# Two attention phases of a hybrid layer: score units in another order, and inverse roots spread over partitions by transposes

## The chip, the cores and the metric

The kernel runs on one core of a Trainium2 chip. The metric is the device time of one execution in microseconds (us); the time of a kernel is the median of its runs. The engines are called as in the profile: PE (TensorE matmuls), PEld (its weight loads), DVE (VectorE), ACT (ScalarE), POOL (GpSimd) and SP (SyncE, which issues the DMAs).

## The reference

One decoder layer over 16 meta tokens and 1024 real tokens, float32: a half feed-forward network, a token mixer, a second half feed-forward network. The mixer has two causal attentions of 8 heads each, and the change is in these two alone:

```python
fq = rms_norm(split_heads(fq, FOX_HEADS), fox_q_norm)      # "fox": head dim 64
fk = rms_norm(split_heads(fk, FOX_HEADS), fox_k_norm)
o_fox = merge_heads(block_causal_attention(fq, fk, fv, log_f_cum)) @ w_branch_fox
...
q = rms_norm(q, mla_q_norm)                                # "mla": 64 + 32 rotary dims
k = rms_norm(k, mla_k_norm)
...
q = jnp.concatenate([q[..., :MLA_NOPE_DIM], rope(q[..., MLA_NOPE_DIM:], cos, sin)], axis=-1)
o_mla = merge_heads(block_causal_attention(q, k, v)) @ w_branch_mla
```

Softmax attention is `softmax(mask(q k^T * scale [+ forget terms])) v`; `rms_norm` multiplies by the inverse root of the mean square of a head's row.

## The kernel before

The layer is written as phases that follow one another: feed-forward network 1, a forget-gate phase, `fox_attention_phase`, `latent_attention_phase` (called MLA here), a gate phase and feed-forward network 2. Each engine has its own program of instructions in order, written out by hand, and engines wait for each other with semaphores (`wait`, `upto`). Float32 products are made of three matmuls on a high and a low part of each operand (`hi`, `lo`).

**Score units.** The scores of a head stand transposed, keys on partitions, queries along the free dimension. A unit is one tile of 128 keys (`kt`, 0 to 8) against one half of the queries (`c`, 0 or 1, 512 queries each), cut to the queries that may see these keys. So a head has `NW` = 14 units of unequal width `n`: for c = 0 widths 512, 400, 272, 144, 16 (kt 0 to 4), for c = 1 widths 512 five times (kt 0 to 4), then 400, 272, 144, 16 (kt 5 to 8). `ST_UNITS` is the list of them, and before it is in just this order. Both phases walk the list with index `w`.

For each unit: PE makes the scores (fox: `scores_open`, `scores_close`, L1921 to L1933; MLA: `scores`, L2435 to L2445; plus a mask matmul if the tile is on the diagonal), ACT takes the exponential (L1811, L2314), DVE rounds it to `p_hi` (L2091, L2601), POOL subtracts to get `p_lo` (L1733, L2250; in fox DVE does so itself for each fourth unit, `w % LO_DVE == 3`, L2094), and PE weighs the values with three matmuls (`weigh`, L1948 to L1950, L2459 to L2461) into the bank `OB[c]`, where a row of ones gives the denominator too. Fox has three score buffers and PE weighs unit w-3 at step w; MLA has two and weighs unit w-2 at step w. The first unit of a half (kt = 0) starts its bank, the last (`LAST_OF[c]`) closes it; some steps later ACT takes logarithm and exponential of the denominators (`rden`, L1817/L1819, L2320/L2322) and DVE multiplies (`o_fox` L2102, `o_mla` L2591).

**Fox** works on pairs of heads (4 pairs). A pair is first projected (6 units `u` of q and k, three groups of tokens, and 3 of v, L73 to L75), its maxima are found (`maxima`, L1905, DVE reduces them, L2048), then come its 2 x 14 score units.

**MLA** works on 8 heads, and preparation of head h+1 is woven into the 14 steps of head h: at steps 0 to 5 PE makes the projection `products(u)` (L2363 q, L2366 k), then the step's scores, then `weigh`, then `sums(u)` (L2376, sums of squares; waits for ACT's squares L2286/L2288) and, a step later, `broadcast(u)`. At steps 8 to 12 it makes the 14 maxima of the next head (L2418, reduced by DVE at L2554, two banks in turn), at step 13 it turns them and makes the values (L2398). The code of `prepare`:

```python
if w < NU:
    sums(p, h, w)
if 1 <= w <= NU:
    broadcast(p, h, w - 1)
maxima(p, h, w, 2)
```

**Inverse roots.** After `sums`, DVE scales (`ms`, L2514), ACT takes logarithm and exponential (L2295, L2297), POOL makes a Newton step of four small instructions (L2236 to L2242; fox L1714 to L1722). The root stands with tokens on partitions and is needed along the free dimension, the same on all partitions: `broadcast(u)` multiplies the column, repeated 128 times, by the identity `g.ident`, once for each of three tiles of 128 tokens (fox L1876, where POOL has written the repeated columns out in `r_wide`; MLA L2387, where the column is read with a stride of zero). ACT copies the result to `rs`, DVE scales q or k with it (L2027; L2525 to L2538) and they are split into hi and lo (L2545).

Of the kernel before, what the change touches and what calls it, by code (L numbers as in the profile page):

```python
# [23 lines left out]
P = 128  # L24
# [4 lines left out]
T = META + SEQ  # L29
# [35 lines left out]
REAL_TOKENS = [(META, 512), (META + 512, 512)]  # L65
# [1269 lines left out]

ST_UNITS = []
for _c, (_q0, _n) in enumerate(REAL_TOKENS):
    for _kt in range(9):  # L1340
        _a = max(_q0, P * _kt)
        if _a < _q0 + _n:
            ST_UNITS.append((_c, _kt, min(P * _kt, T - P), _a, _q0 + _n - _a))
NW = len(ST_UNITS)
LAST_OF = [max(w for w in range(NW) if ST_UNITS[w][0] == c) for c in range(2)]

# [240 lines left out]
def fox_attention_phase(nc, g):  # L1587
# [15 lines left out]
    with ExitStack() as s:  # L1603
# [12 lines left out]
        ms, r0, nt = sb("ms", [P, 2, 3 * NH]), sb("r0", [P, 2, 3 * NH]), sb("nt", [P, 2, 3 * NH])  # L1616
# [9 lines left out]
        PROJ, SUM, BC = (bank[0], bank[1], bank[4], bank[5]), bank[2], bank[6:8]  # L1626
# [201 lines left out]
        def _(pe):  # L1828
            def pair(p, last=False):
# [37 lines left out]
                def broadcast(u):  # L1867
                    c = units[u][1]
                    wait(pe, newton, p, 4 * NU, 4 * u + 4)
                    if u < 2:  # L1870
                        wait(pe, o_done, p, 4, 0)
                    else:
                        wait(pe, rs_done, p, NU, u - 1)
                    for i, off in enumerate(QK_TILES[c]):
                        r = r_wide[:, u % 2, NH * i:NH * i + NH, :].rearrange("p a b -> p (a b)")
                        last = nc.tensor.matmul(BC[u % 2][:, off:off + P], r, g.ident[:, :], start=True, stop=True)  # L1876
                    last.then_inc(bc_ready, 1)

                def values(b):
# [236 lines left out]
def latent_attention_phase(nc, g):  # L2116
# [14 lines left out]
    V_TILES = (range(0, 5), range(5, 9))  # L2131
    MAXIMA_FROM = NU + 2
    TURN_STEP, V_STEP = NW - 1, NW - 1
    FINISH_0, FINISH_1 = 7, 2

    ROPE_ROWS, SWAPPED = slice(NOPE, MLA_D), slice(MLA_D, P)
    with ExitStack() as s:
# [209 lines left out]
        def _(pe):  # L2347
# [32 lines left out]
            def broadcast(p, h, u):  # L2380
                upto(pe, newton, 4 * NU, p, h, 4 * u + 4)
                if u == 0:
                    upto(pe, v_done, 2, p, h, 0)
                else:
                    upto(pe, rs_done, NU, p, h, u)
                for i, off in enumerate(QK_TILES[units[u][1]]):
                    last = nc.tensor.matmul(BC[:, off:off + P], r0[:, u % 2, i:i + 1].broadcast_to([P, P]),  # L2387
                                            g.ident[:, :], start=True, stop=True)
                last.then_inc(bc_ready, 1)

            def values(p, h, b):
# [623 lines left out]
```

## Time and profile before

| | |
|---|---|
| median of 3 runs | 2602.05 us (2597.78 to 2606.18) |
| the profiled execution's own time | 2598.46 us |
| its span in the trace | 2596.3 us |
| mean granted clock of TensorE | 0.958 of full speed |
| PE / DVE / ACT / POOL busy | 94% / 55% / 37% / 21% of the span |

The own time is that of the execution that the profile shows; the span reaches from its first to its last instruction in the trace. The fox phase takes about the stretch from 780 to 1190 us, the MLA phase from 1190 to 1560 us. A head of MLA is one step list of 14; heads start at 1235.7, 1275.1, 1320.7, 1362.3, 1408.1, 1451.0, 1496.9 and 1539.1 us (the close of their first unit), and the last has no preparation beside it.

### The profile page before, as it was taken

Reading aid. Unit: us, or ns where it says so; the run is one execution under the profiler, and the core shown is the slowest. Engines: PE = TensorE matmul, PEld = TensorE weight load, DVE = VectorE, ACT = ScalarE, POOL = GpSimd, SP = SyncE. Lnnn points to the kernel's source line nnn. Section 1 sums busy time; section 2 is a strip of 40 time slices with the busy share of each in tenths; the row PEclk is TensorE's granted clock in tenths of the full one; section 3 lists DMA queues with packets and bytes.
Section 4 is the critical chain, followed back from the end, with each engine's and each line's share of the span. In section 5 each row is a group of like instructions: output and inputs, shape, how many; then the busy total and the mean of one; then the engine's idle time right before and its main releaser. Section 6 shows DMA issues by size and latency. Waiting matters only on the chain. (4 is left out here: it accounts for less than half of the span.)

```text
span 2596.3 us, 37171 instructions
## 1 busy us (share of the span) xinstructions
PE 2433.0 (94%) x14204; PEld 2152.8 (83%) x14204; DVE 1418.0 (55%) x2006; ACT 948.2 (37%) x1578; POOL 557.8 (21%) x655
## 2 busy tenths in 40 slices
PE   6999999999959999978999998999998999999999
PEld 6899999999958888976777777888876888887887
DVE  7665655565456567544666662111466666655553
ACT  5333333333344445432444443111334333334332
POOL 0023300000023344231444444222310333000000
PEclk8999999999979999987998998999999999999999
DMA  4365632565230000010000002111433566326653
GB/s 183 121 209 196 209 114 95 214 227 188 101 130 1 26 26 0 1 33 7 7 7 4 3 1 81 48 49 41 163 113 104 180 221 232 133 87 255 211 197 111
DMA packets 125908, 281.13 MB, mean 108 GB/s; under 512 B 9456, under 2 KB 56432, under 8 KB 122432
## 3 DMA queue, kind: packets, MB, share of 16 engines
q1 hardware_dynamic: 125760, 279.10, 31.0%
q8 instruction: 99, 1.62, 0.3%
q14 instruction: 49, 0.40, 0.0%
HBM read 198.60 MB, written 80.33 MB: 107 GB/s over the span
## 5 line engine op out<-in xcount | busy, mean ns | idle before, releaser
L1068 DVE TENSOR_TENSOR f_w_lo<-f_rw,f_w_hi 128x1024 fp32r<-128x1024 f32 x154 | 203.1, 1319 | 218.7 <-ACT f_w_hi L590 218.6
L833 PE MATMUL f_ps<-u_hi,f_w_hi 128*128 128x260 f32 (+1 forms) x1056 | 283.9, 323 | 26.5 <-DVE f_w_lo L1068 13.6
L833 PE MATMUL f_ps<-u_hi,f_w_lo 128*128 128x260 f32 (+1 forms) x1056 | 282.4, 322 | 0.0
L833 PE MATMUL f_ps<-u_lo,f_w_hi 128*128 128x260 f32 (+1 forms) x1056 | 282.4, 322 | 0.0
L590 ACT CAST f_w_hi<-f_rw 128x1024 fp32r<-128x1024 f32 x154 | 161.3, 1047 | 165.1 <-PE f_ps L833 148.7
L833 PE MATMUL f_ps<-f_far_hi,f_w_hi 128*128 128x260 f32 (+1 forms) x792 | 211.8, 322 | 8.7 <-DVE f_ev L1084 8.7
L833 PEld LDWEIGHTS f_ps<-u_hi,f_w_hi 128*128 128x128 f32 x1056 | 178.0, 192 | 43.1 <-DVE f_w_lo L1068 15.4
L833 PE MATMUL f_ps<-f_far_lo,f_w_hi 128*128 128x260 f32 (+1 forms) x792 | 210.9, 321 | 0.0
L833 PE MATMUL f_ps<-f_far_hi,f_w_lo 128*128 128x260 f32 (+1 forms) x792 | 210.8, 321 | 0.0
L833 PEld LDWEIGHTS f_ps<-u_lo,f_w_hi 128*128 128x128 f32 x1056 | 177.7, 191 | 14.2
L833 PEld LDWEIGHTS f_ps<-u_hi,f_w_lo 128*128 128x128 f32 x1056 | 177.6, 191 | 14.1
L73 PE MATMUL f_ps<-u_hi,f_w_hi 128*128 128x512 f32 x384 | 151.5, 394 | 9.4 <-POOL f_w_lo L2659 9.4
L75 PE MATMUL f_ps<-u_lo,f_w_hi 128*128 128x512 f32 x384 | 151.1, 393 | 0.0
L74 PE MATMUL f_ps<-u_hi,f_w_lo 128*128 128x512 f32 x384 | 151.1, 393 | 0.0
L833 PEld LDWEIGHTS f_ps<-f_far_hi,f_w_hi 128*128 128x128 f32 x792 | 132.8, 191 | 19.9 <-issue 9.6
L833 PEld LDWEIGHTS f_ps<-f_far_lo,f_w_hi 128*128 128x128 f32 x792 | 132.5, 190 | 10.6
L833 PEld LDWEIGHTS f_ps<-f_far_hi,f_w_lo 128*128 128x128 f32 x792 | 132.4, 190 | 10.4
L2761 DVE TENSOR_TENSOR f_sg<-f_ps,f_sg 128x512 f32<-128x512 f32 x32 | 22.1, 692 | 212.2 <-PE f_ps L75 203.4
L2250 POOL TENSOR_TENSOR mla_p_lo<-mla_p,mla_p_hi 128x512 fp32r<-128x512 f32 (+4 forms) x112 | 105.6, 943 | 69.5 <-DVE mla_p_hi L2601 69.5
L73 PE MATMUL fox_bank<-u_hi,fox_w_hi 128*128 128x384 f32 (+1 forms) x288 | 98.6, 342 | 16.1 <-DVE fox_w_lo L2007 15.9
L636 ACT CAST f_w_hi<-f_rw 128x1408 fp32r<-128x1408 f32 x36 | 49.5, 1376 | 171.6 <-PE f_ps L858 136.8
L2659 POOL TENSOR_TENSOR f_w_lo<-f_gt_raw,f_w_hi 128x1024 fp32r<-128x1024 f32 x27 | 66.5, 2467 | 198.0 <-ACT f_w_hi L2679 198.0
(385 smaller groups left out, 5987.1 us busy)
## 6 DMA issues: line engine op xcount, KB each, us to landing
f_rw<-in_gu SPq DMA_DIRECT2D x88, 512.0 KB, 4.4
f_rw<-kept_dsum SPq DMA_DIRECT2D x32, 704.0 KB, 4.9
f_rw<-kept_hid SPq DMA_DIRECT2D x33, 520.0 KB, 5.7
f_rw<-in_down SPq DMA_DIRECT2D x24, 704.0 KB, 4.1
f_rw<-kept_hid SPq DMA_DIRECT2D x33, 512.0 KB, 5.5
f_gt_raw<-in_gate SPq DMA_DIRECT2D x24, 512.0 KB, 3.5
h_in<-in_wd SPq DMA_DIRECT2D x11, 1024.0 KB, 7.2
kept_dsum<-h_in SPq DMA_DIRECT2D x44, 256.0 KB, 3.1
```

What stands on the lines that cost most here:

```text
L73: nc.tensor.matmul(out, w_hi, x_hi, start=first, stop=False)
L74: nc.tensor.matmul(out, w_lo, x_hi, start=False, stop=False)
L75: return nc.tensor.matmul(out, w_hi, x_lo, start=False, stop=last)
L590: nc.scalar.copy(slot(w_hi, st), src).then_inc(whi_done, 1)
L636: nc.scalar.copy(s_buf(near_hi, far_hi, w_hi, n), s_raw(n)).then_inc(shi_done, 1)
L833: last = nc.tensor.matmul(out[:, b, 0:N], w[:, c], u[:, b * N:(b + 1) * N], start=(j < 3 and k == 0 and i == 0), stop=(k == 3 and i == 2), ...
L1068: nc.vector.tensor_tensor(slot(w_lo, st), src, slot(w_hi, st).bitcast(F32), ALU.subtract).then_inc(wlo_done, 1)
L2250: nc.gpsimd.tensor_tensor(p_lo[:, w % 2, 0:n], p32[:, w % 2, 0:n], p_hi[:, w % 2, 0:n].bitcast(F32), ALU.subtract).then_inc(plo_done, 1)
L2659: nc.gpsimd.tensor_tensor(w_lo[:, j, :], raw[:, j, :], w_hi[:, j, :].bitcast(F32), ALU.subtract).then_inc(wlo_done, 1)
L2761: ins = nc.vector.tensor_tensor(sg[:, slot, :], bank[base + which][:, :], sg[:, slot, :], ALU.mult)
```

## The change

1. `ST_UNITS` gets a written-out order. Widths by step, before: 512, 400, 272, 144, 16, 512, 512, 512, 512, 512, 400, 272, 144, 16. After: 512, 400, 272, 512, 144, 512, 16, 512, 16, 512, 144, 512, 272, 400. `LAST_OF` goes from (4, 13) to (6, 13), and with it the finish of half 0: in MLA from step 7 to step 9 (`FINISH_0`), in fox from steps 8 and 22 of the 28 to steps 10 and 24.
2. Both `broadcast` functions issue `nc.tensor.transpose` of the repeated column in place of `nc.tensor.matmul` of it with the identity.

```diff
+ST_ORDER = [(0, 0), (0, 1), (0, 2), (1, 0), (0, 3), (1, 1), (0, 4), (1, 2), (1, 8), (1, 3), (1, 7), (1, 4), (1, 6), (1, 5)]
 ST_UNITS = []
-for _c, (_q0, _n) in enumerate(REAL_TOKENS):
-    for _kt in range(9):
-        _a = max(_q0, P * _kt)
-        if _a < _q0 + _n:
-            ST_UNITS.append((_c, _kt, min(P * _kt, T - P), _a, _q0 + _n - _a))
+for _c, _kt in ST_ORDER:
+    _q0, _n = REAL_TOKENS[_c]
+    _a = max(_q0, P * _kt)
+    ST_UNITS.append((_c, _kt, min(P * _kt, T - P), _a, _q0 + _n - _a))
...
-                        last = nc.tensor.matmul(BC[u % 2][:, off:off + P], r, g.ident[:, :], start=True, stop=True)
+                        last = nc.tensor.transpose(BC[u % 2][:, off:off + P], r, g.ident[:, :])
...
-    FINISH_0, FINISH_1 = 7, 2
+    FINISH_0, FINISH_1 = LAST_OF[0] + 3, 2
...
-                    last = nc.tensor.matmul(BC[:, off:off + P], r0[:, u % 2, i:i + 1].broadcast_to([P, P]),
-                                            g.ident[:, :], start=True, stop=True)
+                    last = nc.tensor.transpose(BC[:, off:off + P], r0[:, u % 2, i:i + 1].broadcast_to([P, P]),
+                                               g.ident[:, :])
```

## Rows read from the trace of the kernel before

**Rows 1.** The page's head and part 1: busy us of each engine.
```profile
span 2596.3 us, 37171 instructions
PE 2433.0 (94%) x14204; PEld 2152.8 (83%) x14204; DVE 1418.0 (55%) x2006; ACT 948.2 (37%) x1578; POOL 557.8 (21%) x655
```

**Rows 2.** Windows: length; PE, PEld, DVE, ACT, POOL busy; clock; DMA.
```profile
949.00:1004.50 55.50, 52.45 (x353) 50.42 (x352) 24.89 (x57) 23.50 (x60) 12.79 (x29) 1.00 0.09 29
915.20:949.00 33.80, 30.71 (x156) 25.04 (x154) 30.88 (x53) 18.94 (x39) 20.09 (x19) 0.95 0.01 1
1275.10:1320.70 45.60, 41.98 (x227) 34.59 (x226) 29.34 (x65) 19.23 (x51) 18.30 (x38) 0.89 0.02 4
1320.70:1362.30 41.60, 39.08 (x228) 32.13 (x226) 29.77 (x65) 19.30 (x51) 18.57 (x38) 0.96 0.02 6
```

**Rows 3.** MLA head 4, timeline of all engines, steps 3 and 5 to 8.
```profile
1419.18 0.48 ACT L2288 ACTIVATE ksq<-mla_bank 64x384 f32<-64x384 f32 x1
1419.71 0.83 PE L2376 MATMUL mla_bank<-ones,ksq 96*128 96x1 f32 x6 [1.14 <-ACT ksq L2288]
...
1427.45 0.22 POOL L2250 TENSOR_TENSOR mla_p_lo<-mla_p,mla_p_hi 128x16 fp32r<-128x16 f32 x1
1430.76 1.26 POOL L2250 TENSOR_TENSOR mla_p_lo<-mla_p,mla_p_hi 128x512 fp32r<-128x512 f32 x1
1430.77 1.55 DVE L2531 TENSOR_TENSOR mla_by_sin<-mla_x,sin 32x272 f32<-32x272 f32 x1
1430.85 0.93 PE L2387 MATMUL mla_bank<-ident,mla_r 128*128 128x128 f32 x6 [0.67 <-POOL mla_r L2242]
...
1431.54 0.48 PE L2435 MATMUL mla_bank<-mla_q_hi,mla_k_lo 96*128 96x512 f32 x1
1433.77 0.34 PE L2418 MATMUL mla_bank<-mla_k_hi,mla_q_hi 96*128 96x144 f32 x1 [0.59 <-DVE mla_k_lo L2545]
1437.21 0.45 PE L2418 MATMUL mla_bank<-mla_k_hi,mla_q_hi 96*128 96x400 f32 x1 [1.31 <-DVE mla_mpart L2554]
```

**Rows 4.** By source line: who waited for fox's `p_lo` of POOL (L1733): us, times.
```profile
  PEld fox_bank L1948: 15.8, 35
  PE fox_bank L1948: 8.9, 22
```

**Rows 5.** By source line: duration ns minimum/median/maximum, first and last start, forms.
```profile
L1876 PE MATMUL fox_bank<-ident,fox_r_wide x144: 271/275/421, 786.3 to 1081.5; 128*128 128x128 f32 x144
L2387 PE MATMUL mla_bank<-ident,mla_r x288: 275/275/562, 1198.4 to 1519.8; 128*128 128x128 f32 x144
L1888 PE MATMUL fox_bank<-ident,fox_vt x36: 270/272/282, 819.0 to 1092.7; 128*128 128x128 f32 x36
```

**Rows 6.** PE's timeline: start, length, line, count: a broadcast, three transposes, what follows.
```profile
1411.84 0.91 PE L2387 MATMUL mla_bank<-ident,mla_r 128*128 128x128 f32 x6
1412.59 1.46 PE L2363 MATMUL mla_bank<-cq,mla_w_head 128*128 128x384 f32 x4
...
912.08 0.50 PE L1888 MATMUL fox_bank<-ident,fox_vt 128*128 128x128 f32 x3
912.33 0.47 PE L1921 MATMUL fox_bank<-fox_q_both,fox_k_both 128*128 128x512 f32 x1
```

**Rows 7.** Groups by form: fox's `p_lo` of 512 columns, on POOL and on DVE.
```profile
L1733 POOL TENSOR_TENSOR fox_p_lo<-fox_p,fox_p_hi 128x512 fp32r<-128x512 f32 x36 | 48.3, 1350 | 34.3 <-DVE fox_p_hi L2091 34.3
L2094 DVE TENSOR_TENSOR fox_p_lo<-fox_p,fox_p_hi 128x512 fp32r<-128x512 f32 x12 | 15.1, 1257 | 0.4
```

**Rows 8.** PE's timeline at the start of the program: its first transposes.
```profile
11.33 3.43 PE L898 MATMUL f_ps<-ident,ld_xin 128*128 128x128 f32 x16 [1.34 <-DVE h_in L1197]
...
15.28 1.97 PE L898 MATMUL f_ps<-ident,ld_xin 128*128 128x128 f32 x16
```

**Rows 9.** Windows: sixteen more transposes, and 3 us after them.
```profile
24.30:28.50 4.20, 3.77 (x16) 3.01 (x17) 4.20 (x7) 4.20 (x9) 0.00 (x0) 0.50 0.47 178
31.50:34.00 2.50, 2.50 (x23) 2.50 (x23) 2.50 (x4) 0.00 (x0) 0.00 (x0) 1.00 1.03 382
```

## The prediction, made before the change was run

> **What bounds the kernel now.** I read the page's part 1 first [rows 1]: PE is busy 94% of the span, so time goes down where PE has less to issue or waits less. The change touches two phases alone, so next come windows cut at their stages [rows 2]. In fox's projection PE is busy 52.45 of 55.50 us and the others less than half of that: PE sets that stage. In fox's attention (28 units of a pair) DVE is busy 30.88 of 33.80 us and PE 30.71: two engines at their limit. In a steady head of MLA PE is busy 39.08 to 41.98 us of 41.60 to 45.60, DVE under 30: PE again, with holes. The two MLA rows also show a second thing: the same work took 45.60 us at a mean granted clock of 0.89 and 41.60 at 0.96. The level falls to 1.2 GHz for short stretches after PE had holes, and back.
>
> The holes come third, from the timeline of one head [rows 3]. At step 3 `sums` waited 1.14 us for ACT's square, which stood behind the finish of the head before. At step 6 `broadcast` waited 0.67 us for the Newton step. At step 8 (its first and third maximum) PE waited 0.59 us for DVE's `k_lo` and 1.31 us for a reduction. These last two are one backlog: DVE's `by_sin` took 1.55 us, it started together with a `p_lo` of 512 columns on POOL (1.26 us) and got through only after it; then a queue of splits, scalings and reductions is late, all DVE. Steps 6 to 8 lose 0.67 + 0.59 + 1.31 = 2.57 us of PE. In fox the waits are before `weigh`: 8.9 us for matmuls and 15.8 us for weight loads over the phase, all on POOL's `p_lo` [rows 4]; the two overlap, so they are between 8.9 and 24.7 us, 2 to 6 us per pair.
>
> **Transposes in place of matmuls.** A float32 matmul with the identity has two records for each tile in the trace (144 for the 4 x 6 x 3 = 72 tiles of fox; 288 for the 8 x 6 x 3 = 144 of MLA), a float32 transpose of the same 128x128 one (36 for the 4 x 9 tiles of `values`), and a record is as long in both, 275 against 272 ns [rows 5]. What PE's queue feels is the spacing from start to next start: six records of a broadcast hold PE for 0.75 us (1411.84 to 1412.59 [rows 6]) or 0.69 us (1430.85 to 1431.54 [rows 3]), three transposes for 0.25 us (912.08 to 912.33 [rows 6]). The difference, 0.44 to 0.50 us, has in it a slower first record, which may well stay. Three records of six at 0.69 us are 0.345 us. Bounds: nothing (if the repeated column costs a transpose as much as the second record did) and 0.50 us. I take 0.34, the value that only removes records.
> - Fox: 24 calls, all between dense projection matmuls, PE-bound: 24 x 0.34 = 8.2 us.
> - MLA: 48 calls, 16.3 us. The call of u = 5 is in step 6, where PE waits for POOL anyway, those of u = 2 and 3 stand next to the hole of step 3, and when steps get shorter DVE (busy about 29 us of each head [rows 2], much of it in steps 1 to 8) has less room. I count two thirds: 11 us.
>
> **The order in MLA.** Total work is the same, it only moves among the steps. Steps 6 and 8 change from 512 to 16 columns. POOL's `p_lo` there falls from 1.26 to 0.22 us [rows 3], so two of the pieces that DVE collides with nearly vanish, and its rounding shortens too; DVE's product for the finish leaves step 7 for step 9. With 2 x 1.04 us of POOL less to collide with, I reckon DVE's backlog about 2 us smaller. Against it: step 6 covers the Newton step with scores of 16 columns where it had 512, an estimated 0.3 us less (the 512 ones are three or four matmuls, the short ones are held up by their weight loads), and its wait of 0.67 us grows by that and by what broadcasts save; step 3 gets a 512 unit where it had 144, but its hole of 1.14 us takes that at no cost, as ACT's queue sets it; units of 272 and 400 are now weighed in steps 0 and 1 of the next head, where PE has no hole. Of the 2.57 us I take 1.5 per head, the 2 us less what steps 0, 1 and 6 give back, over 7 prepared heads 10.5 us; bounds 0 and 2.57 (18 us). What waits behind a late `p_hi` on DVE is POOL's `p_lo`, then PE's `weigh`; a long unit (1.26 us of POOL) still has a long one's `weigh` and a short step between its scores and its own `weigh`, and its neighbours' `p_lo` is short, so I add no wait. The last head and the preparation of the first: 1.5 us.
>
> **The order in fox.** Before, the run of five or six 512 units has PE waiting and the short units do not. Alternated, with three buffers, the short ones give POOL time to catch up. Two costs: the fourth units (DVE's own `p_lo`) were 144, 512, 272, 400, 512, 512, 16 wide and are now 512, 512, 512, 400, 512, 512, 400, 992 columns more, about two of 512. On DVE that is 2 x 1.257 us [rows 7] per pair, in a stage where DVE is busy 91%: at worst 10 us over four pairs. POOL is freed of 2 x 1.350. And half 1 of the second head starts at its step 3, where it stood at step 5, with the finish of the first head's half 1 at step 3 in both, so `weigh` may have to wait for that finish; I count nothing for it beyond the 10 us. Between a gain of all waits (up to 24.7) and a loss of 10, I take 4 us gain, as POOL's share and DVE's nearly cancel and the rest is smoothing.
>
> The Trainium skill (SBUF — State Buffer, "SBUF: two separate sides") says the pair of ports that DVE and GpSimd share is an exclusive lock for a whole instruction. The 1.55 us of `by_sin` [rows 3] agree. By this rule fox's stage could gain only what moves off the shared pair, and smoothing would give little; my 4 us would be about as small.
>
> **The sum.** 8.2 + 11 + 10.5 + 1.5 + 4 = 35.2 us off the profiled execution's own 2598.46 us: 2563.3. The median of the runs is 3.6 us above that execution, so 2566.9, say 2567 us.
>
> **Rivals.**
> 1. The order gives nothing back: holes move to ACT's and POOL's chains (step 6's wait grows as reckoned, fox's DVE eats its part). Only transposes count: 2602.05 - 19.2 = 2583 us. For it: the waits of steps 3 and 6 are latency, not load. Against: the 1.31 us are plain DVE load.
> 2. All holes close and the low clock with them: transposes in full 24.5, order in MLA 18, fox 10, and three heads at 0.89 come to 0.96, 3 x 4.0 = 12: 64.5 us, 2538 us.
> 3. The transposes are no shorter (the stride-zero or wide operand costs it): 2602.05 - 16 = 2586 us.
> 4. Slower: PE's clock. After steps that stream few columns (16-wide units next to short transposes) the level falls in more stretches. The price is in the two heads of rows 2: 4.0 us for 0.07 of clock. To eat the 35 us takes nine such falls. If each of 7 heads falls by 0.10 (5.7 us, 40 in all) and fox's four attentions by 0.07 (34/43 of 4.0 each, 13 in all), the time is 2567 + 53 = 2620 us; it decides from 35 us on. The rows on transposes alone go both ways: sixteen took 3.43 us from 11.33, the next sixteen 1.97 us from 15.28, so the level had risen after nothing but transposes [rows 8]; but sixteen at 24.30 to 28.50 left it at 0.50, and it was 1.00 only behind the matmuls after them [rows 9]. The Trainium skill (TensorE: Matmul & The Clock Gate, "Part 4: PE-mode transpose") says that transposes don't count as PE work for the clock; the first of these rows is against it, the second for it.
> 5. All is given back, no change: 2602 us.
>
> **Chances and range.** The forecast (2555 to 2579) 0.47, rival 1 0.21, rival 2 0.12, rival 3 0.07, rival 4 0.07, rival 5 0.06. A measurement of this kernel tells about 0.3% (8 us) from no change. Faster 0.47 + 0.21 + 0.12 + 0.07 = 0.87; same 0.06; slower 0.07. The range takes in rivals 1 and 3 with their bounds and the near side of rival 2: 2542 to 2592; outside are most of rival 2's far half, rival 4 and rival 5.
>
> **What would show it.** Records of L1876 and L2387 halve to 72 and 144 and three of them hold PE about 0.33 us. In an MLA head the 1.31 and 0.59 us before L2418 shrink below 0.5 each, the wait for POOL before L2387 at step 6 grows to about 1 us, the 1.14 us at step 3 stays near 0.9. A head's window is about 39 to 40 us. In fox, `weigh` waits less for L1733 but DVE is busy still over 90%. The prediction is wrong if heads keep 42 us or more, if the granted clock in them sinks under 0.89, or if fox's attention grows beyond 34 us.

## The result, and the profile after

| | before | after |
|---|---|---|
| median of 20 runs each, same chip | 2598.10 us (2588.20 to 2606.52) | 2606.89 us (2599.72 to 2616.52) |
| ratio, with 95% interval | | 1.0034 [1.0023, 1.0044] |
| the profiled execution's own time | 2598.46 us | 2604.38 us |
| its span | 2596.3 us | 2602.3 us |
| mean granted clock of TensorE in it | 0.958 | 0.947 |

The change makes the kernel 0.34% slower, 8.8 us: far below 2%, but with an interval clear of 1. 35 us less had been forecast. One run of the whole study (2809.82 us, of e8 below) is left out as disturbed: its mean granted clock was 0.806. The page's head and part 1 after:

```profile
span 2602.3 us, 36741 instructions
PE 2428.6 (93%) x13988; PEld 2148.1 (83%) x13988; DVE 1415.8 (54%) x2006; ACT 942.7 (36%) x1578; POOL 552.4 (21%) x655
```

Against [rows 1] PE has 216 records fewer, the 72 + 144 that were to go, and it is busy only 4.4 us less. The prediction's 0.34 us for each of the 72 calls would be 24 us; that it is 4.4 us means that other records got longer. The granted clock, below, says why.

**Where the time went.** From fox's first projection matmul to its last `weigh` the phase took 359.5 us before (769.7 to 1129.2) and 353.3 after (769.2 to 1122.5): 6.2 us less. The MLA phase, from there to the first matmul of the next phase, before and after:

```profile
1129.20:1568.50 439.30, 380.31 (x2045) 309.18 (x2043) 249.95 (x546) 175.87 (x433) 159.21 (x312) 0.89 0.04 13
```

```profile
1122.50:1576.70 454.20, 390.63 (x1899) 318.45 (x1898) 254.50 (x546) 172.07 (x433) 163.86 (x312) 0.81 0.04 12
```

It is 14.9 us longer, with 146 PE records less and 10.3 us more of PE busy time, at a clock of 0.81 instead of 0.89. The whole loss is in this phase.

**Fox, windows of the trace after** (length; PE, PEld, DVE, ACT, POOL busy; clock; DMA share and GB/s), the attention and the projection that answer to [rows 2]:

```profile
911.90:943.70 31.80, 28.22 (x154) 23.24 (x154) 29.11 (x53) 18.39 (x39) 17.24 (x20) 1.00 0.01 2
944.20:1000.70 56.50, 52.09 (x331) 49.39 (x331) 26.24 (x57) 23.50 (x60) 13.10 (x29) 0.97 0.08 28
```

The attention is 2.0 us shorter, at a clock of 1.00 where it had 0.95; the projection with its maxima is 1.0 us longer with 22 PE records less, and its clock has sunk from 1.00 to 0.97.

**MLA, windows after**: heads 1 and 4 (counted from 0, as in the prediction).

```profile
1272.30:1316.60 44.30, 40.56 (x210) 33.45 (x208) 29.83 (x65) 18.59 (x51) 19.24 (x38) 0.85 0.02 4
...
1406.70:1456.20 49.50, 47.57 (x209) 40.03 (x208) 29.93 (x65) 19.19 (x51) 19.19 (x38) 0.69 0.02 5
```

The seven prepared heads before took 39.5, 45.6, 41.6, 45.8, 43.0, 45.8 and 42.2 us; after, 42.9, 44.3, 45.0, 45.1, 49.5, 44.6 and 44.1. No head is at the 39 to 40 us of the forecast. Head 4 has as many records as the others and its DVE, ACT and POOL are as busy; PE alone is 7 us busier, at a clock of 0.69. The same stretch cut in two, head 1 after: steps 0 to 5, then 6 to 12.

```profile
1272.30:1292.30 20.00, 17.63 (x108) 13.73 (x106) 13.01 (x28) 11.14 (x33) 9.81 (x25) 1.00 0.03 8
1292.30:1311.80 19.50, 18.13 (x74) 15.71 (x75) 15.07 (x34) 5.87 (x15) 7.63 (x11) 0.65 0.00 0
```

and head 2 before, cut at the same steps:

```profile
1320.70:1340.80 20.10, 18.87 (x123) 15.44 (x122) 12.74 (x28) 11.55 (x34) 8.21 (x26) 1.00 0.03 10
1340.80:1357.80 17.00, 15.71 (x77) 12.81 (x75) 15.17 (x33) 6.41 (x14) 9.65 (x11) 0.90 0.00 1
```

Steps 6 to 12 hold the loss against this head: 19.50 us at 0.65 after, 17.00 us at 0.90 before. (Head 2 is one of the faster heads before; against head 1 before, 45.6 us at 0.89, head 1 after is 1.3 us shorter.) The clock has two levels in these traces, 1.00 (2.4 GHz) and 0.50 (1.2 GHz), so a mean gives the time at the low one: length x (1 - clock) / 0.5. That is 13.65 us of the 19.50 after and 3.4 us of the 17.00 before. In head 1 after it comes in two pieces, with the high level between them:

```profile
1293.80:1297.20 3.40, 3.23 (x9) 2.68 (x10) 3.18 (x7) 1.30 (x3) 1.80 (x3) 0.51 0.00 0
1297.20:1300.70 3.50, 3.20 (x21) 2.54 (x20) 3.50 (x9) 1.14 (x3) 1.75 (x2) 0.99 0.00 0
1300.70:1310.90 10.20, 10.20 (x36) 9.14 (x35) 6.35 (x14) 2.25 (x6) 2.98 (x3) 0.50 0.00 0
```

After, the first low stretch begins at step 6 in six of the seven heads. In head 4, the longest, it begins behind the wait of step 3 and lasts 30.7 us without a break:

```profile
1420.10:1450.80 30.70, 30.46 (x108) 26.36 (x106) 20.64 (x44) 10.03 (x27) 11.78 (x21) 0.50 0.00 0
```

**The holes, PE's timeline after** (start, length, line; in brackets what PE waited for), head 1: a broadcast and what follows it, then what stood behind the waits of steps 3, 5 and 6.

```profile
1276.30 0.52 PE L2387 MATMUL mla_bank<-ident,mla_r 128*128 128x128 f32 x3
1276.65 1.46 PE L2363 MATMUL mla_bank<-cq,mla_w_head 128*128 128x384 f32 x4
1283.89 0.83 PE L2376 MATMUL mla_bank<-ones,ksq 96*128 96x1 f32 x6 [1.42 <-ACT ksq L2288]
1290.95 0.83 PE L2376 MATMUL mla_bank<-ones,ksq 96*128 96x1 f32 x6 [0.95 <-ACT ksq L2288]
1293.97 0.90 PE L2387 MATMUL mla_bank<-ident,mla_r 128*128 128x128 f32 x3 [1.07 <-POOL mla_r L2242]
```

Three transposes hold PE's queue for 0.35 us (1276.30 to 1276.65) where six records held it for 0.75 [rows 6]. The wait at step 3 is 1.42 us (head 4 before: 1.14 [rows 3]), a second one of 0.95 us has come up at step 5, and the one at step 6 has grown to 1.07 us from 0.67. The holes at step 8 [rows 3] are gone (at most 0.50 us is left, in head 3). So within about 10 us (1283.89 to 1293.97) PE stands still three times, 3.4 us in all, and at the end of it (1293.80) the level falls. 13.65 of the 17.1 us from there to 1310.90 are at the low level, although PE is busy for 16.6 of them.

The sources by line, and who waited for fox's `p_lo` of POOL (L1733):

```profile
L1876 PE MATMUL fox_bank<-ident,fox_r_wide x72: 270/273/328, 785.7 to 1075.6; 128*128 128x128 f32 x72
L2387 PE MATMUL mla_bank<-ident,mla_r x144: 272/302/476, 1191.4 to 1523.1; 128*128 128x128 f32 x144
...
  PEld fox_bank L1948: 14.5, 26
  PE fox_bank L1948: 11.3, 24
```

A transpose is one record, as long at the high level as each of the two before (minimum 272 ns against 275 [rows 5]; MLA's median of 302 ns has the low level in it); 72 and 144 are left. Fox's waits for `p_lo` are 14.5 and 11.3 us where they were 15.8 and 8.9 [rows 4]: the order took none of them away.

### The profile page after: what moved, and what is told of

The parts are those of the page before. It is cut to its first block and busy times, and to the rows that moved or that the text cites. A ratio compares the mean times of both kernels' runs of the same rounds, so it can differ in the third digit from the quotient of the medians.

```text
span 2602.3 us, 36741 instructions
## 1 busy us (share of the span) xinstructions
PE 2428.6 (93%) x13988; PEld 2148.1 (83%) x13988; DVE 1415.8 (54%) x2006; ACT 942.7 (36%) x1578; POOL 552.4 (21%) x655
## 5 line engine op out<-in xcount | busy, mean ns | idle before, releaser
L1068 DVE TENSOR_TENSOR f_w_lo<-f_rw,f_w_hi 128x1024 fp32r<-128x1024 f32 x154 | 194.0, 1260 | 221.2 <-ACT f_w_hi L590 221.2
L833 PE MATMUL f_ps<-u_hi,f_w_hi 128*128 128x260 f32 (+1 forms) x1056 | 283.9, 323 | 26.0 <-DVE f_w_lo L1068 13.2
L833 PEld LDWEIGHTS f_ps<-u_hi,f_w_hi 128*128 128x128 f32 x1056 | 178.0, 192 | 42.1 <-DVE f_w_lo L1068 14.7
L833 PEld LDWEIGHTS f_ps<-u_lo,f_w_hi 128*128 128x128 f32 x1056 | 177.8, 192 | 14.4
L833 PEld LDWEIGHTS f_ps<-f_far_hi,f_w_lo 128*128 128x128 f32 x792 | 132.3, 190 | 10.2
L2250 POOL TENSOR_TENSOR mla_p_lo<-mla_p,mla_p_hi 128x272 fp32r<-128x272 f32 (+3 forms) x112 | 108.9, 972 | 99.0 <-DVE mla_p_hi L2601 98.4
L636 ACT CAST f_w_hi<-f_rw 128x1408 fp32r<-128x1408 f32 x36 | 49.5, 1376 | 171.4 <-PE f_ps L858 136.4
```

The source lines that it names most:

```text
L636: nc.scalar.copy(s_buf(near_hi, far_hi, w_hi, n), s_raw(n)).then_inc(shi_done, 1)
L833: last = nc.tensor.matmul(out[:, b, 0:N], w[:, c], u[:, b * N:(b + 1) * N], start=(j < 3 and k == 0 and i == 0), stop=(k == 3 and i == 2), ...
L1068: nc.vector.tensor_tensor(slot(w_lo, st), src, slot(w_hi, st).bitcast(F32), ALU.subtract).then_inc(wlo_done, 1)
L2250: nc.gpsimd.tensor_tensor(p_lo[:, w % 2, 0:n], p32[:, w % 2, 0:n], p_hi[:, w % 2, 0:n].bitcast(F32), ALU.subtract).then_inc(plo_done, 1)
```

## The experiments

Every run of every kernel lists its span and the mean granted clock, which gives a second measure beside the ratio. Within one kernel, a run with 0.001 more clock has a span about 1.5 us shorter (slope -1.48 over 94 runs of the kernel before, -1.54 over 20 of the changed one; the other kernels, with 6 to 12 runs each, give -0.9 to -2.4). So a kernel's span can be read **at equal clock**, here at 0.956, from the straight line through its own runs; where that line would rest on few or distant runs (e10 to e12, marked ~) a common slope of 1.5 is used. For after, e2, e5 and e7 all runs have a clock under 0.956, so their value is extrapolated. The runs of before are three sets, one beside each group of experiments, and they agree: 2597.9, 2598.3 and 2599.0 at equal clock. 0.001 of the clock over 2600 us is 5.2 us at the low level, so a microsecond at 1.2 GHz costs about 0.29 us on average. In a single head it can cost more: the heads of [rows 2] have 10.0 and 3.3 us of it and differ by 4.0 us, 0.6 each, of which 2.9 us are PE's busy time and the rest longer holes.

The theories when the experiments began: **clock** (rival 4 of the prediction: the change lets the level fall), against **order** (the new order moves its holes and costs what the transposes save) and, within clock, whether it is the *kind* of operation that matters or the *amount* that PE streams. Each table row below is one kernel: median span and clock of its runs, span at 0.956, ratio to the kernel before.

| kernel | runs | span, us | clock | at 0.956 | ratio [95%] |
|---|---|---|---|---|---|
| before | 94 | 2596.6 | 0.957 | 2598.3 | 1 |
| after | 20 | 2604.8 | 0.945 | 2587.3 | 1.0034 [1.0023, 1.0044] |
| e1 order only | 12 | 2593.0 | 0.9605 | 2600.5 | 0.9997 [0.9978, 1.0016] |
| e2 transposes only | 12 | 2595.1 | 0.9465 | 2581.4 | 1.0006 [0.9984, 1.0027] |
| e3 after, filled | 12 | 2597.9 | 0.9545 | 2594.3 | 0.9994 [0.9974, 1.0013] |
| e4 before, filled | 12 | 2595.1 | 0.9595 | 2600.2 | 0.9993 [0.9981, 1.0006] |
| e5 fp32r matmul, old order | 12 | 2603.6 | 0.9395 | 2578.9 | 1.0025 [1.0012, 1.0038] |
| e6 transposes twice, old order | 12 | 2598.3 | 0.956 | 2597.8 | 1.0007 [0.9993, 1.0020] |
| e7 fp32r matmul, new order | 8 | 2609.9 | 0.941 | 2587.4 | 1.0045 [1.0029, 1.0061] |
| e8 new order, MLA with matmuls | 11 | 2597.0 | 0.954 | 2594.4 | 0.9997 [0.9979, 1.0015] |
| e9 transposes, 272-column fill | 12 | 2589.6 | 0.956 | 2588.9 | 0.9968 [0.9951, 0.9985] |
| e10 transposes, 2-column fill | 12 | 2602.8 | 0.9435 | ~2584 | 1.0018 [1.0001, 1.0034] |
| e11 new order, filled more | 12 | 2592.1 | 0.961 | ~2600 | 0.9985 [0.9966, 1.0003] |
| e12 fox new order, MLA old, filled | 6 | 2582.4 | 0.9635 | ~2594 | 0.9931 [0.9906, 0.9956] |

The spread of the runs leaves some 2 us of doubt on a number at equal clock, and more where it is extrapolated: 0.2 in the slope moves e2's by 1.9 us. Each window shown below is of one execution, which need not be the median one: the spans of the profiled executions are 2589.1 us for e1 and e2, 2586.9 for e4, 2602.7 for e6.

### e1: the order alone

```diff
-                        last = nc.tensor.transpose(BC[u % 2][:, off:off + P], r, g.ident[:, :])
+                        last = nc.tensor.matmul(BC[u % 2][:, off:off + P], r, g.ident[:, :], start=True, stop=True)
...
-                    last = nc.tensor.transpose(BC[:, off:off + P], r0[:, u % 2, i:i + 1].broadcast_to([P, P]),
-                                               g.ident[:, :])
+                    last = nc.tensor.matmul(BC[:, off:off + P], r0[:, u % 2, i:i + 1].broadcast_to([P, P]),
+                                            g.ident[:, :], start=True, stop=True)
```

> The new order with the broadcasts as matmuls. Clock theory, order variant (the 16-wide units at steps 6 and 8 leave PE too little to do and the clock falls): low clock in the MLA phase stays near the changed kernel's 150 us (before: 81), the MLA phase is 8 us or more longer than before, total 2600 to 2615. Clock theory, transpose variant (transposes don't hold the level up, or the wait that they lengthen does it): low clock in MLA back near 80 us, total 2588 to 2598, faster than before. Schedule theory (the loss is waits, not clock): holes at steps 3, 5 and 6 as in the changed kernel, and heads near 44 us even where the clock is full.

Measured: 2595.13 us, ratio 0.9997 [0.9978, 1.0016]. At equal clock 2600.5 us against 2598.3: the order gives nothing. That is what the clock theory forecast for the case that the transposes, and not the order, let the level fall. The seven heads of MLA, windows of the profile of before and of e1:

```profile
1235.70:1539.10 303.40, 279.92 (x1568) 228.62 (x1566) 204.72 (x454) 133.35 (x347) 130.02 (x266) 0.93 0.01 4
```

```profile
1235.20:1529.50 294.30, 272.50 (x1567) 221.54 (x1565) 208.05 (x454) 132.50 (x347) 131.22 (x266) 0.96 0.02 4
```

This stretch is 9 us shorter, but at a clock of 0.96 instead of 0.93: 23.5 us at 1.2 GHz instead of 42.5. Heads with the same single low stretch of 3.4 us took 41.6, 43.0 and 42.2 us before and 41.9 to 42.7 in e1. The hole at step 8 is closed in e1, and step 5 is 0.8, step 13 0.36 and step 1 0.2 us longer for it; the last head with the tail behind it went from 19.7 to 21.9 us. In fox the attentions of most pairs are shorter, yet one of e1's, that of pair 2, has this stretch in it:

```profile
1003.00:1023.50 20.50, 20.31 (x67) 17.90 (x68) 12.22 (x28) 7.48 (x16) 6.94 (x9) 0.50 0.00 0
```

For these 20.50 us of it PE is at 1.2 GHz without a break and busy for 20.31, and the whole attention took 38.2 us against 32.3 for pair 1. The profiles of e3 and e8 have one such attention too and that of e7 two, those of before and after none. The runs of e1 spread over 24 us (2589.44 to 2613.28), in two groups some 16 us apart. The profiled execution belongs to the fast group, its long attention notwithstanding, so what makes the slow group is open.

### e2: the transposes alone

The edit is the two `nc.tensor.transpose` calls of the change on the kernel before, the list `ST_UNITS` as it was.

> The old order with the broadcasts as transposes. Order variant: low clock near 80 us in MLA, heads 1 to 2 us shorter than before, total 8 to 16 us under before. Transpose variant: low clock in MLA well over 81 us, towards 150, total the same as before or up to 10 us slower. In fox the stretch from a pair's first projection to its first maximum should be 0.8 us shorter as in the changed kernel, with the wait before the first maximum growing from 1.8 to 2.8 us.

Measured: 2597.28 us, ratio 1.0006 [0.9984, 1.0027]. The clock is 0.9465 where before has 0.957. At equal clock the span is 16.9 us under before (2581.4 against 2598.3): by this measure the transposes save what they were said to save, and the clock takes it back. This is the case that the expectation called the transpose variant. The seven heads, and inside one head steps 3 to 5 and the stretch after them:

```profile
1233.60:1532.50 298.90, 273.50 (x1441) 219.59 (x1439) 207.90 (x454) 131.14 (x348) 133.19 (x266) 0.89 0.02 4
1315.00:1327.20 12.20, 10.27 (x65) 7.84 (x64) 6.62 (x13) 6.84 (x19) 5.56 (x15) 1.00 0.04 15
1327.20:1341.00 13.80, 13.80 (x55) 11.62 (x55) 9.59 (x20) 6.47 (x20) 5.26 (x15) 0.55 0.00 1
```

In 12.20 us PE was busy 10.27 at the high level, with 1.93 us of holes; then come 13.80 us at 0.55, nearly all at 1.2 GHz, with PE busy all the time. Here the holes stand just ahead of the low stretch and not in it. The hole ahead in another head (1.14 us before [rows 3]):

```profile
1412.87 0.83 PE L2376 MATMUL mla_bank<-ones,ksq 96*128 96x1 f32 x6 [1.93 <-ACT ksq L2288]
```

PE-bound steps show the saving by itself: steps 1 and 2 of a head took 3.52 and 3.50 us before and 3.12 and 3.10 in e2, 0.40 us less for each broadcast, where 0.34 had been taken.

Stages that run at the same level in both profiles give less than 17 us, though. In fox the stretch from the first projection matmul to the first score matmul that closes a unit, all at the high level, took 53.1 us in pairs 1 and 2 before and 52.1 in e2: 1.0 us a pair where 2.0 were forecast. MLA heads with a single low stretch of 3.4 us took 41.6 us (head 2 before) against 41.2 (head 1 of e2) where it lies at step 6, and 43.0 against 42.1 (head 4 of both) where it lies at step 3: 0.4 and 0.9 us where 1.6 were forecast. Over four pairs and seven heads that is an estimated 7 to 10 us. How much of the 17 us the transposes themselves are worth stays open between the two readings.

### e3 and e4: matmuls in the holes, after and before

Both put matmuls whose results nobody reads into the places where PE waits. BC is the bank of the broadcasts, free until the next one.

```diff
+            FILL = {3: 8, 5: 4, 6: 6}     # e4: {3: 6, 6: 3}
...
+            def fill(p, h, w):
+                if w in FILL:
+                    upto(pe, rs_done, NU, p, h, w - 1)
+                    for _ in range(FILL[w]):
+                        nc.tensor.matmul(BC[:, 0:272], g.ident_r[:, :], g.masks[:, 0:272], start=True, stop=True)
...
             def prepare(p, h, w):
+                fill(p, h, w)
```

> The changed kernel with extra matmuls of 272 columns whose result is overwritten, in MLA at steps 3 (8), 5 (4) and 6 (6), where PE waits: 18 per head and 144 in all, about 17 us of PE work that is added and nothing removed. Clock theory: low clock in MLA falls from 150 us to under 90, and although work is added the total is 8 to 16 us under the changed kernel. Schedule theory: low clock may change, the total doesn't fall, or it grows by up to 5 us.

> The kernel before with the same kind of extra matmuls at MLA steps 3 (6) and 6 (3). Clock theory: low clock in the MLA phase falls from 81 us towards 45, heads at 0.89 come to 0.96 or more, total 5 to 15 us under before. Schedule theory: no gain, 0 to 4 us slower.

Measured: e3 2600.02 us, 0.9994 [0.9974, 1.0013]; e4 2597.24 us, 0.9993 [0.9981, 1.0006]. With 144 matmuls more than the changed kernel (18 for each of eight heads, 126 of them in the seven windows below), e3 is 7 us under it and its clock is 0.9545 instead of 0.945: work was added and the time fell, as only the clock theory has it, though 8 to 16 us had been expected. On before, the same trick raises the median clock by 0.0025 and gains nothing that can be told, where 5 to 15 us had been expected. In the profiled execution of e4 its seven heads took 293.0 us at 0.98, 10 us less than before's, but that execution is the shortest of the twelve.

```profile
1235.80:1543.10 307.30, 290.61 (x1567) 235.39 (x1565) 208.19 (x454) 128.49 (x347) 134.53 (x266) 0.90 0.02 4
```

These are e3's seven heads; the changed kernel has there

```profile
1229.30:1544.90 315.60, 289.99 (x1441) 239.76 (x1439) 208.08 (x454) 129.44 (x348) 134.71 (x266) 0.82 0.02 4
```

so 61 us at 1.2 GHz (0.20 / 0.5 of 307.30) against 114. PE is as busy in both, 290.6 and 290.0 us, with 126 matmuls more in e3.

### e5 and e7: not transposes, but as few records

A matmul of fp32r operands has one record, as a transpose has. e5 is e2, and e7 the changed kernel, with such matmuls in the place of the transposes. The inverse roots are rounded to fp32r in both, so a part of the computation has less precision.

```diff
-        r_wide = sb("r_wide", [P, 2, 3 * NH, FOX_D])
+        r_wide = sb("r_wide", [P, 2, 3 * NH, FOX_D], F32R)
...
-                        last = nc.tensor.transpose(BC[u % 2][:, off:off + P], r, g.ident[:, :])
+                        last = nc.tensor.matmul(BC[u % 2][:, off:off + P], r, g.ident_r[:, :], start=True, stop=True)
...
-                nc.gpsimd.tensor_tensor(r, r, t, ALU.mult).then_inc(newton, 1)
+                nc.gpsimd.tensor_tensor(r_r[:, u % 2, :], r, t, ALU.mult).then_inc(newton, 1)
...
-                    last = nc.tensor.transpose(BC[:, off:off + P], r0[:, u % 2, i:i + 1].broadcast_to([P, P]),
-                                               g.ident[:, :])
+                    last = nc.tensor.matmul(BC[:, off:off + P], r_r[:, u % 2, i:i + 1].broadcast_to([P, P]),
+                                            g.ident_r[:, :], start=True, stop=True)
```

> The old order; each broadcast tile is one ordinary matmul of fp32r operands (the roots are rounded to fp32r before it, which lowers their precision): one record a tile as with a transpose, but not a transpose. Mode theory (transposes don't hold the clock up): mean clock of the runs back at 0.956 to 0.960 and the median span 12 to 20 us under before (2597): 2577 to 2585. Work theory (fewer records leave PE too empty, whatever they are): clock 0.945 to 0.949 as with transposes, median span within 3 us of theirs (2595).

> The changed kernel's order with one fp32r matmul a tile (roots rounded to fp32r). Mode theory: clock near 0.958, median span 2578 to 2588, that is some 20 us under the changed kernel (2605). Work theory: clock 0.945, span 2600 to 2608.

Measured: e5 2605.71 us, 1.0025 [1.0012, 1.0038], clock 0.9395; e7 2612.05 us, 1.0045 [1.0029, 1.0061], clock 0.941. Ordinary matmuls, and the clock sinks as with transposes, or a little more (e2 0.9465, after 0.945). Both runs fell on the side of the work theory but beyond its numbers: it had e5 within 3 us of e2, and it came out 8.5 us longer. The runs of e5 have clocks from 0.936 to 0.943 and those of e2 from 0.933 to 0.952, so whether such a matmul holds the level less than a transpose isn't settled. e5's line by source, and its seven heads as a window:

```profile
L2388 PE MATMUL mla_bank<-ident_r,mla_r_r x144: 273/415/473, 1198.0 to 1526.1; 128*128 128x128 f32 x144
```

```profile
1237.90:1545.70 307.80, 291.28 (x1441) 237.68 (x1439) 207.78 (x454) 133.62 (x347) 134.68 (x266) 0.83 0.01 4
```

The median of 415 ns says the same as the window's 0.83: about half of these records ran at the low level. By the times of the low stretches they are 75 of the 144. So the falling level is not a property of the transpose.

### e6: the transposes, each done twice

The order is the old one. Each broadcast goes over its three tiles twice, so PE has as many records as before (144 and 288), all of them transposes.

```diff
-                    for i, off in enumerate(QK_TILES[c]):
+                    for i, off in enumerate(QK_TILES[c] * 2):
+                        i %= 3
...
-                for i, off in enumerate(QK_TILES[units[u][1]]):
+                for i, off in enumerate(QK_TILES[units[u][1]] * 2):
+                    i %= 3
```

> The old order with each transpose issued twice, so PE has as many broadcast records as before. Mode theory: the clock stays at 0.947 or lower though PE holds as long as before, and the time is 10 to 20 us over before. Work theory: clock 0.956 and time within 4 us of before.

Measured: 2600.48 us, 1.0007 [0.9993, 1.0020], clock 0.956. That is before in all three: ratio, clock, and span at equal clock (2597.8 against 2598.3). Transposes, record for record, keep the mean clock as well as the matmuls that they replace; half as many of either do not. With e5 and e6 the loss goes with the amount of work taken out and not with its kind. The level is not the same in each head: in the profiled execution, 4 us longer than the median one, the seven heads took 307.4 us at 0.91, and heads 2 and 4 have low stretches of 13.7 and 17.1 us.

### e8: fox as changed, MLA with matmuls

The second of e1's two edits alone, on the changed kernel.

> The changed kernel with only MLA's broadcasts back as matmuls; fox keeps transposes and both keep the new order. If the low clock comes from MLA's transposes alone, the clock goes from 0.945 to 0.958 or more and the median span to 2586 to 2594, better than before (2597) and than the order alone (2593).

Measured: 2599.10 us, 0.9997 [0.9979, 1.0015], clock 0.954. Putting MLA's 144 second records back makes the changed kernel 7.8 us faster by span (2604.8 to 2597.0). Had MLA's transposes been the only cause, the clock would have come to 0.958 and the span under 2594, by the expectation; the rest of the way to e1 (0.9605) goes with fox's transposes, the only difference between e8 and e1.

```profile
1236.80:1536.10 299.30, 278.33 (x1567) 228.32 (x1565) 208.39 (x454) 132.38 (x347) 130.85 (x266) 0.93 0.02 4
```

Its seven heads are 16.3 us shorter than the changed kernel's, with 126 of those records in them: 42 us at 1.2 GHz and not 114.

### e9 and e10: the same fill, wide and narrow

e9 is e2 with fill in steps 3 (8 matmuls) and 6 (6 matmuls), written as in e3. e10 is e9 with each of them cut to two columns; records and weight loads are the same in number.

```diff
-                        nc.tensor.matmul(BC[:, 0:272], g.ident_r[:, :], g.masks[:, 0:272], start=True, stop=True)
+                        nc.tensor.matmul(BC[:, 0:2], g.ident_r[:, :], g.masks[:, 0:2], start=True, stop=True)
```

> The old order, transposes, and in MLA 8 extra matmuls of 272 columns at step 3 and 6 at step 6, where PE waits (about 1 and 0.75 us). Clock theory (the emptied holes let the clock fall, whatever kind of record was removed): clock from 0.9465 (transposes alone) to 0.955 or more, median span 2580 to 2588 (before 2597), though 112 matmuls are added. If the clock needs the work in the dense steps and not in the holes: clock stays under 0.950 and the span is within 3 us of 2595.

> As the run before, with the extra matmuls 2 columns wide: as many records and weight loads, next to no columns streamed. If columns streamed hold the clock: it stays at 0.945 to 0.949 and the span near 2595 to 2600. If records or weight loads do: same as the 272-column fill.

Measured: e9 2591.71 us, 0.9968 [0.9951, 0.9985], clock 0.956; e10 2604.91 us, 1.0018 [1.0001, 1.0034], clock 0.9435. The fill in the groups by form (count, busy us, mean ns), first e9, then e10:

```profile
L2470 PE MATMUL mla_bank<-masks,ident_r 128*128 128x272 f32 x112 | 18.8, 311 | 0.5 <-ACT mla_rs L2303 0.5
```

```profile
L2470 PE MATMUL mla_bank<-masks,ident_r 128*128 128x2 f32 x112 | 17.4, 274 | 0.5 <-ACT mla_rs L2303 0.5
```

PE's timeline at step 3 of head 1, e9:

```profile
1287.12 1.16 PE L2470 MATMUL mla_bank<-masks,ident_r 128*128 128x272 f32 x8
1288.95 0.83 PE L2376 MATMUL mla_bank<-ones,ksq 96*128 96x1 f32 x6 [0.67 <-ACT ksq L2288]
```

and e10:

```profile
1284.79 0.94 PE L2470 MATMUL mla_bank<-masks,ident_r 128*128 128x2 f32 x8
1286.62 1.43 PE L2376 MATMUL mla_bank<-ones,ksq 96*128 96x1 f32 x6 [0.88 <-ACT ksq L2288]
```

The windows of the seven heads, e9 and then e10:

```profile
1232.90:1533.50 300.60, 275.12 (x1539) 221.71 (x1538) 207.48 (x454) 128.65 (x347) 133.72 (x266) 0.94 0.02 4
```

```profile
1236.10:1543.80 307.70, 292.61 (x1539) 240.37 (x1537) 208.44 (x454) 132.74 (x348) 133.71 (x266) 0.86 0.02 4
```

The 112 fills are busy for 18.8 and 17.4 us, nearly alike, though eight of them at the high level hold PE for 1.16 and 0.94 us, and leave holes of 0.67 and 0.88 us behind them. The wide ones bring e2's clock back to that of before (36 us at 1.2 GHz in the seven heads); the narrow ones leave it where e2 has it, or lower (86 us; in e2 66). e9 met the clock that was expected and is 1.6 us over the range of spans; e10 lies just beyond the numbers for the case that columns count, and far from those for the case that records do. Busy time as the profile counts it doesn't tell the two apart: 14 matmuls of 272 columns a head brought the clock back here, and 14 of two columns did not.

### e11 and e12: what beats both

e11 is the changed kernel with `FILL = {3: 10, 5: 6, 6: 8}` and, in fox, six such matmuls at step 3 of a pair, ahead of its first `weigh`. e12 has these six, the new order in fox alone, the old order in MLA with e9's fill, and transposes in both.

```diff
+                    if w == 3:
+                        wait(pe, v32_done, p, 3, 3)
+                        for _ in range(6):
+                            nc.tensor.matmul(OB[1][:, 0:272], g.ident_r[:, :], g.masks[:, 0:272],
+                                             start=True, stop=True)
...
     NU = 6
+    ST_UNITS = [(c, kt, min(P * kt, T - P), max(q0, P * kt), q0 + n - max(q0, P * kt))
+                for c, (q0, n) in enumerate(REAL_TOKENS) for kt in range(9) if max(q0, P * kt) < q0 + n]
+    LAST_OF = [4, 13]
```

> The changed kernel with extra matmuls in MLA at steps 3 (10), 5 (6), 6 (8) and in fox 6 at the first head's step 3, where its attention's low clock starts. Clock theory: clock 0.955 to 0.962, span 2585 to 2595, and fox attentions of 38 us no longer appear. Otherwise 2598 to 2605.

> Fox in the new order, MLA in the old one, transposes in both, extra matmuls in MLA at steps 3 (8) and 6 (6) and in fox at step 3 (6). Sum of the stage gains so far: fox 353 to 356 us (before 360), MLA 355 to 360 (before 367): median span 2578 to 2590, the best of all. If fox's new order costs in its tail and projection what it wins in attention, no better than the old order filled.

Measured: e11 2594.25 us, 0.9985 [0.9966, 1.0003]; e12 2584.65 us, 0.9931 [0.9906, 0.9956] over six runs, the fastest kernel of the study, 14 us under before and 22 under the changed one. The spans and clocks of both lie within what was expected. e12's seven heads:

```profile
1232.30:1527.30 295.00, 272.83 (x1539) 220.11 (x1537) 207.40 (x454) 128.77 (x347) 133.76 (x266) 0.95 0.02 4
```

No fox attention of the two profiles ran long (31.4 to 31.8 us in pairs 0 to 2, 29.6 in pair 3), which agrees with the wide matmuls at its start, though each is one execution. e12 differs from e9 by fox's new order and fox's fill together, and their intervals just overlap. The lead of 7.2 us is one of clock: at equal clock e12 is not under e9 (~2594 against 2588.9). Nor is it all fox's, since the code of MLA is the same in both and its seven heads took 295.0 us here and 300.6 in e9. What fox's order adds is not settled. e11 shows what fill costs: at equal clock it has lost the 11 us that the changed kernel had gained.

## Why the prediction was wrong

**The step that failed** is the sum: it takes PE work and PE holes off at a constant clock. The clock's term stood at nothing in it; it measured 18 us. The mechanism was there as rival 4, with a chance of 0.07 and "decides from 35 us on". The clock fell by 0.012 in the mean (0.957 to 0.945); at the slope of 1.54 us that is 18 us, half of those 35. It decided all the same, because at equal clock only 11 us of the 35.2 were gained (2598.3 to 2587.3): the terms for the order failed as well. The order and the transposes read one by one at equal clock (e1 +2, e2 -17) come to -15, so up to 4 us of that is doubt or interplay. The clock was also not counted in the forecast itself, although the heads of [rows 2] had shown that one of them loses 4.0 us to it and the holes of steps 3 and 6 were known to stay or to grow. A smaller fault: the sum ends on the median of three runs, 2602.05 us, which over twenty was 2598.10. Two of the prediction's own signs of being wrong came: the heads took 42.9 to 49.5 us, and the clock in them was 0.82. The third, a fox attention beyond 34 us, did not.

**Transposes, fox 8.2 and MLA 11, 19.2 us**: right at equal clock by the line through the runs (16.9 us in e2), and right for one call where PE is the bound (0.35 us in the queue, 0.40 in a PE-bound step); but stages at the same level in both profiles show 7 to 10 us, so that the total is right is not shown. In fox, six calls a pair shorten the stretch from the first projection to the first maximum only from 36.3 to 35.5 us: 0.94 us of a wait ahead of the maxima comes back, as that wait ends with DVE's `k_both` (pair 2, after):

```profile
982.68 0.33 PE L1905 MATMUL fox_bank<-fox_k_hi,fox_q_hi 66*128 66x144 f32 x1 [2.75 <-DVE fox_k_both L2039]
```

It was 1.81 us. Behind it the level falls for 3.4 us, and the maxima up to the turn take 14.4 us where they took 13.2 in pairs 1 and 2. In these two pairs nothing is left of the saving; over all four the stretch from the first projection to the first close is 2.7 us shorter (217.4 to 214.7) where 8.2 were forecast.

**Order in MLA, 10.5 + 1.5 us**: wrong. The holes of step 8 closed as forecast, and the time went to steps 5, 13 and 1 and to the end of the last head (+2.2 us where 1.5 had been taken off). e1 at equal clock: +2 us for both orders together. The step that failed here is counting the backlog at step 8 as PE time that is won when the hole closes. Why the time comes back in other steps no run shows; that DVE's work has to be done by the end of the head in any case is one reading. The wait at step 3 did not stay near 0.9 us but went to 1.4 to 1.7, and that of step 6 came to 1.07 to 1.26 as forecast. The same grew in e1, where the broadcasts are matmuls, only to 0.8 and 0.86, with 0.8 to 0.9 at step 3: the holes that precede the low level come from the order and the transposes together.

**Order in fox, 4 us**: the attention of a pair fell from 33.07, 33.70 and 34.71 us to 31.49, 31.83 and 31.84. (These are pairs 0 to 2.) About 1 us of that is the clock, which was low for 3.4 to 6.8 us in each before and for none after (e1 with 3.4 us of it: 32.34). The tail behind the attention rose from 2.20, 2.49 and 2.19 us to 3.37, 3.40 and 3.40, since the last units weighed are 512, 272 and 400 wide and were 272, 144 and 16. That term was missing; it eats most of the rest. From the first close to the last `weigh`, over four pairs, 141.5 us became 138.0: 3.4 us, close to the 4, but by luck, since after has 13.6 us less of the low level there. Pair 1, with 3.4 us of it in both, took 35.78 us before and 35.57 in e1: 0.2 us for the order. The waits for `p_lo` hardly moved, 24.7 us together before and 25.8 after. The stage's DVE share is 29.11 of 31.80 us, 92%, as said.

**The two rules cited.** The Trainium skill (TensorE: Matmul & The Clock Gate, "Part 4: PE-mode transpose") says that a transpose doesn't count as busy PE for the clock in the way that a matmul does. The runs here don't bear it out: matmuls of the same count in their place had a lower clock (0.9395 against 0.9465, 0.941 against 0.945), and twice the transposes had the clock of before. The prediction had left open which way that rule goes, from [rows 8] and [rows 9]. Its reading of [rows 8], a level that rose after transposes alone, is worked out from their lengths; the granted clock of that stretch (11.33 to 14.40 us) reads 1.00 already. In e5 the level sank without a transpose, so the rule wasn't needed for it. On the shared ports of DVE and GpSimd (the Trainium skill, SBUF — State Buffer, "SBUF: two separate sides"), fox's nearly unmoved waits for `p_lo` agree with the estimate that smoothing gives little there; no run here tests the rule itself.

**Shown and open.** Shown: the loss is the clock's (e3, e9 and e8 bring it back by adding work), it goes with the work taken out and not with the kind of operation (e5, e6, e7), fill of 272 columns brings the clock back where fill of two does not (e9 against e10), and neither the order nor the transposes alone are slower. Open: how much the transposes are worth at equal clock, and why the level stays low for 10.2 us, or 30.7 in head 4, while PE is busy, and for most of an attention of fox in some executions. Nothing here tells what ends such a stretch.

## What to carry over

Where PE is the bound but has holes, check the granted clock of each stage before and after taking PE work out: holes with less work around them can cost the level for many times their length (3.4 us of waits, then 13.65 us at 1.2 GHz, in head 1). Here the change gained 11 us at equal clock and lost 18 by the clock. Reading a change's worth at equal clock from the spread of the runs helps to tell the mechanism from what the clock does with it, but hold it against stages that ran at the same level, which here gave less. When a hole can't be closed, matmuls of 272 columns whose results nobody reads were worth it on the old order (e9: 112 added, 0.3% faster); two-column ones were not, and the more of them, the more they cost at equal clock (e11).

## What the runs showed of the hardware

- Adding 112 matmuls of 272 columns raised the mean granted clock from 0.9465 to 0.956 and shortened the kernel; 112 of two columns, busy for 17.4 us against 18.8, did not (0.9435).
- A low stretch, once begun, went on with PE busy nearly all the time: 13.80 of 13.80 us at a clock of 0.55 in e2, 20.31 of 20.50 us of one fox attention in e1, 30.46 of 30.70 us in head 4 of the changed kernel.
- A float32 transpose, like an fp32r matmul, is one record of about 272 ns where a float32 matmul is two of 275; three transposes hold the queue for 0.35 us against 0.69 to 0.75.
